# Two gate tiles of a hybrid diffusion trunk multiplied in attention, where identity products stood

## The reference

```python
h = rmsnorm(x, p['norms'][0]) * (1.0 + scale1) + shift1
z = h @ p['w_in']
qa, ka, va, ub, vb, qkvc, bc, ac, zc, gates = jnp.split(z, split_idx, axis=-1)
...
o_a = block_attention(qa, k_all, v_all)
o_b = chunk_gmlp(jax.nn.gelu(ub), jax.nn.gelu(vb), p['gmlp_norm'], p['gmlp_ws'], p['gmlp_bs'])
o_c, s_fin = deltanet_mixer(qkvc, bc, ac, zc, p['dn_conv'], p['dn_a_log'], p['dn_dt_bias'], p['dn_norm'], s0)
g_a, g_b, g_c = jnp.split(jax.nn.sigmoid(gates), N_BRANCH, axis=-1)
...
merged = g_a * (o_a @ wb[0]) + g_b * (o_b @ wb[1]) + g_c * (o_c @ wb[2])
```

## Time and profile before

| | us |
|---|---|
| median of 3 executions | 1819.18 (1812.81 to 1821.51) |
| the profiled execution | 1815.65 |
| its span | 1813.5 |
| PE busy | 1755.4 (97%) |
| DVE, ACT, POOL busy | 1020.1, 790.3, 257.7 |

### The profile page before, as it was taken

How to read it: one execution, slowest core, us unless ns; L and a number is a source line. 1 busy time by engine, 2 the same in 40 slices (tenths; PEclk the granted TensorE clock), 3 DMA queues, 4 the chain that set the end, 5 groups by cost and what they waited for, 6 DMA issues and landing times.

```text
span 1813.5 us, 32205 instructions
## 1 busy us (share of the span) xinstructions
PE 1755.4 (97%) x13983; PEld 1462.4 (81%) x13983; DVE 1020.1 (56%) x1379; ACT 790.3 (44%) x1108; POOL 257.7 (14%) x228
## 2 busy tenths in 40 slices
PE   5999999999999999999999999999999999999997
PEld 4889788987979999888898788887978555556885
DVE  2866645444745344326965545545748544345887
ACT  3355732234335233225366523235356433335775
POOL 2620033241000000003500223330002000000001
PEclk9999999999999999999999999999999999999999
DMA  9661152216453434337541323127567988979994
GB/s 359 202 246 59 52 218 71 95 48 231 142 208 105 139 100 132 139 132 284 189 171 53 124 100 118 48 89 237 216 222 259 364 307 319 343 276 389 385 379 197
DMA packets 175189, 351.27 MB, mean 194 GB/s; under 512 B 5161, under 2 KB 60481, under 8 KB 174544
## 3 DMA queue, kind: packets, MB, share of 16 engines
q1 hardware_dynamic: 170880, 334.50, 51.8%
q0 software_dynamic: 4176, 14.82, 2.3%
HBM read 320.46 MB, written 28.84 MB: 193 GB/s over the span
## 4 chain that ended last, share of the span: by engine, by line
PE 81%; DMA 6%; DVE 5%; ACT 4%; issue 2%; POOL 1%; SPq 0%; POOLq 0%; DVEq 0%; ACTq 0%
PE bank L1806 6%; PE bank L1195 6%; PE bank L1197 5%; PE bank L1196 5%; PE bank L1666 3%; PE bank L1668 3%; PE bank L1782 3%; PE bank L1667 3%; PE bank L1235 3%; PE bank L1783 3%; PE bank L1785 3%; PE bank L1237 3%; PE bank L1236 3%; PE bank L1614 2%; PE bank L1119 2%
## 5 line engine op out<-in xcount | busy, mean ns | idle before, releaser
L1965 ACT ACTIVATE ring_split<-ring 128x1024 fp32r<-128x1024 f32 (+2 forms) x84 | 119.2, 1447 | 178.2 <-DMA ring<-in_ffn_w_up 101.8
L1197 PE MATMUL bank<-hT_hi,ring_split 128*128 128x384 f32 x576 | 193.4, 336 | 0.0
L2884 DVE TENSOR_TENSOR ring_split<-ring,ring_split 128x2048 fp32r<-128x2048 f32 (+1 forms) x28 | 73.8, 2670 | 141.5 <-ACT ring_split L1965 141.5
L1195 PE MATMUL bank<-hT_hi,ring_split 128*128 128x384 f32 x384 | 139.8, 364 | 0.7 <-DVE modv L2540 0.5
L1237 PE MATMUL bank<-ring_split,hT_hi 128*128 128x256 f32 x480 | 135.2, 282 | 0.0
L793 DVE TENSOR_TENSOR ring_split<-ring,w_upper_a 128x2048 fp32r<-128x2048 f32 (+2 forms) x54 | 96.4, 1814 | 59.2 <-PE bank L1806 39.4
L1196 PE MATMUL bank<-hT_lo,ring_split 128*128 128x384 f32 x384 | 128.4, 334 | 0.0
L1666 PE MATMUL bank<-hT_hi,ring_split 128*128 128x384 f32 x352 | 119.1, 338 | 0.0
L1668 PE MATMUL bank<-hT_hi,ring_split 128*128 128x384 f32 x352 | 118.6, 337 | 0.0
L1667 PE MATMUL bank<-hT_lo,ring_split 128*128 128x384 f32 x352 | 117.2, 333 | 0.0
L1235 PE MATMUL bank<-w_gran,hT_hi 128*128 128x256 f32 x384 | 107.7, 280 | 1.3 <-ACT ktok L1965 1.3
(11 more groups left out here) (464 smaller groups left out, 4338.4 us busy)
## 6 DMA issues: line engine op xcount, KB each, us to landing
ring<-in_w_in SPq DMA_DIRECT2D x28, 2048.0 KB, 9.3
ring<-in_ada_w SPq DMA_DIRECT2D x24, 2048.0 KB, 8.8
ring<-in_moe_w_down SPq DMA_DIRECT2D x18, 1536.0 KB, 7.7
ring<-in_moe_w_gate SPq DMA_DIRECT2D x26, 1024.0 KB, 6.0
ring<-in_moe_w_up SPq DMA_DIRECT2D x26, 1024.0 KB, 8.7
ring<-in_w_branch SPq DMA_DIRECT2D x8, 1536.0 KB, 11.5
ring<-in_ffn_w_gate SPq DMA_DIRECT2D x11, 1024.0 KB, 5.3
ring<-in_ffn_w_up SPq DMA_DIRECT2D x11, 1024.0 KB, 7.9
```

The costliest lines, as they stand in the source:

```text
L1195: mm(out, hi, hT_hi[:, k], start=k == 0, stop=False)
L1197: last = mm(out, lo, hT_hi[:, k], start=False, stop=k == KT - 1)
L1965: return go(out, in_, ACT.Copy)
```

## The change

`FILL` becomes a table for each pair. In pairs 0 and 1 the spots u1 to u5, uw, ws0 and so0 have one step less each, 8 steps or one tile a pair. The two tiles T_G + 0 and T_G + 1 are multiplied ahead of DeltaNet: 2 steps where layer 0 had 5 identity products and layer 1 none, 6 steps in place of the 8 identity products, and 2 steps in each of `flip(0)` to `flip(3)` in place of 4, 1, 1 and 1 identity products; `flip(4)` loses its one. DeltaNet thus starts with tile 2, pair 1 with tile 9 and pair 2 with tile 16 as before (`G_FIRST`).

ACT makes the upper parts of blocks 0 and 1 ahead of the decay exponentials, block 2 alone ahead of attention, and copies tile 0 there and tile 1 in attention step 5. DVE subtracts blocks 0 and 1 before it normalises the gMLP values and no longer block 0 ahead of the attention loop. Tile 1 goes to bank 1, since bank 0 is in use by attention, and `weigh(4)` waits until bank 1 is read out. SP's text is not touched.

```diff
--- before.py
+++ after.py
@@ -91,9 +91,11 @@
 LAST = len(LEVELS) - 1
 
 
-FILL = ([("head", 8), ("in", 8), ("turn", 6)]
-        + [spot for s in range(1, LAST + 1) for spot in ((f"w{s}", 2), (f"u{s}", 4 if s < LAST else 3))]
-        + [("uw", 3), ("ws0", 3), ("so0", 4), ("ws1", 3)])
+FILL = tuple([("head", 8), ("in", 8), ("turn", 6)]
+             + [spot for s in range(1, LAST + 1) for spot in ((f"w{s}", 2), (f"u{s}", (3 if less else 4) - (s == LAST)))]
+             + [("uw", 3 - less), ("ws0", 3 - less), ("so0", 4 - less), ("ws1", 3)] for less in (1, 1, 0))
+G_EARLY = 2
+G_FIRST = [G_EARLY + sum(units for spots in FILL[:pair] for _, units in spots) // 8 for pair in range(3)]
 MASKED = -30000.0
 
 
@@ -296,8 +298,8 @@
 
         def filled(pair, spot):
 
-            n = 64 * pair
-            for name, units in FILL:
+            n = 8 * G_FIRST[pair]
+            for name, units in FILL[pair]:
                 n += units
                 if name == spot:
                     return n // 8
@@ -611,7 +613,7 @@
 
         def feature_bank(n):
 
-            return B[(n if n < T_G else n + 1) % 2]
+            return B[1 if n == T_G + 1 else (n if n < T_G else n + 1) % 2]
 
         def token_bank(n):
 
@@ -1330,8 +1332,19 @@
                             last = tr(B[b][:, h * P:(h + 1) * P], cv[:, j0 + h, TCOL[t]:TCOL[t] + P])
                         last.then_inc(S["kvt_mm"], 1)
 
-                if layer == 0:
-                    keep_warm(1, 5)
+                nfill = [0]
+
+                def gate_steps(units):
+
+                    for i in range(nfill[0], nfill[0] + units):
+                        n, k = divmod(i, KT)
+                        if k == 0:
+                            wait(pe, "v_lo", layer, 13 + n + 1)
+                            wait(pe, "proj_ev", layer, T_G + n if 0 < n <= G_EARLY else T_G + n - 1)
+                        feature_step(layer, T_G + n, 7 + n // 4, n % 4, k)
+                    nfill[0] += units
+
+                gate_steps(2)
                 wait(pe, "a_ok", layer, 1)
                 pe.wait_ge(cache_in, 48 * (layer + 1))
                 for t in range(NT):
@@ -1352,7 +1365,7 @@
                     last = tr(B[7][:, g * P:(g + 1) * P], wsraw[:, g])
                 last.then_inc(S["tr_mm"], 1)
 
-                keep_warm(1, 8)
+                gate_steps(6)
                 wait(pe, "tr_ev", layer, 6)
                 wait(pe, "v_ok", layer, 1)
                 for t in range(NT):
@@ -1383,8 +1396,8 @@
                     last.then_inc(S["at_s"], 1)
 
                 def flip(i):
-                    if i < 5:
-                        keep_warm(1, 1 if i else 4)
+                    if i < 4:
+                        gate_steps(2)
                     if i:
                         wait(pe, "at_pt", layer, i)
                     for b in range(2):
@@ -1396,6 +1409,8 @@
                 def weigh(i):
                     t, a, x, w = at_step(i)
                     wait(pe, "at_pt", layer, i + 1)
+                    if i == 4:
+                        wait(pe, "proj_ev", layer, T_G + G_EARLY)
                     if i == 8:
                         wait(pe, "at_o", layer, 1)
                     vs = [qkv[:, 0, 768:1024]] if t == 0 else [vcache, qkv[:, 1, 768:1024], qkv[:, 2, 768:1024]]
@@ -1422,18 +1437,9 @@
                     if i >= 3:
                         weigh(i - 3)
 
-                nfill = [0]
-
                 def fill(pair, spot):
 
-                    units = dict(FILL)[spot]
-                    for i in range(nfill[0], nfill[0] + units):
-                        n, k = divmod(i, KT)
-                        if k == 0:
-                            wait(pe, "v_lo", layer, 13 + n + 1)
-                            bank_free(layer, T_G + n)
-                        feature_step(layer, T_G + n, 7 + n // 4, n % 4, k)
-                    nfill[0] += units
+                    gate_steps(dict(FILL[pair])[spot])
                     assert nfill[0] // 8 == filled(pair, spot)
 
                 QUADS = ((0, 0), (1, 1), (0, 1), (1, 0))
@@ -1485,7 +1491,7 @@
                         wait(pe, "at_o", layer, 3)
                     dn_ada = at[("d0", "d1")[pair]] if pair < 2 else ()
                     for n in dn_ada:
-                        bank_free(layer, T_G + 8 * pair + 1)
+                        bank_free(layer, T_G + G_FIRST[pair] + 1)
                         for half in range(2):
                             ada_quad(n, half, 0)
                     if pair:
@@ -2124,6 +2130,8 @@
                     evac(T_UV + t, uB[:, t], ACT.Gelu_apprx_tanh)
                 for m in range(2, 4):
                     upper_w(layer, 6, m)
+                for m in range(2):
+                    upper_w(layer, 7, m)
                 wait(act, "gc_v", layer, 1)
                 go(edec, edec, ACT.Exp)
                 go(egl, egl, ACT.Exp)
@@ -2147,8 +2155,8 @@
                         copy(kTt[:, :, 256 * (i - 3):256 * (i - 2)], v3(B[2 + i][:, :], 2)).then_inc(S["tr_ev"], 1)
                     else:
                         copy(wsT, B[7][:, :]).then_inc(S["tr_ev"], 1)
-                for m in range(3):
-                    upper_w(layer, 7, m)
+                upper_w(layer, 7, 2)
+                evac(T_G, gates[:, 0], width=TOK)
                 go(yhalf, one1, ACT.Exp)
 
                 def mixed(t):
@@ -2176,12 +2184,14 @@
                                accum_out=ars[:, 2 * i + b:2 * i + b + 1]).then_inc(S["at_e"], 1)
                     if i == 0:
                         mixed(2)
+                    if i == 5:
+                        evac(T_G + 1, gates[:, 1], width=TOK)
                     if i >= 7 and i % 4 == 3:
                         t = i // 4 - 1
                         wait(act, "at_pv", layer, 4 * (t + 1))
                         copy(oT[:, 0, :, t * P:(t + 1) * P], v3(B[t % 2][:, :], 4)).then_inc(S["at_o"], 1)
 
-                ngate, nup = [0], [3]
+                ngate, nup = [G_EARLY], [3]
 
                 def gates_of(pair, spot):
 
@@ -2698,6 +2708,7 @@
                 link(v.tensor_copy(gcs, gps[:, :, 0:8]))
                 v.tensor_tensor(edec, gps[:, :, 8:16], gcs, ALU.subtract)
                 v.tensor_copy(egl.rearrange("p t c n -> p t (c n)"), gps[:, :, 16:32]).then_inc(S["gc_v"], 1)
+                lower_gates(2)
                 wait(dve, "v_rt", layer, 1)
                 link(v.reciprocal(vss, vss))
                 for t in range(NT):
@@ -2716,7 +2727,6 @@
                     last.then_inc(S["b_v"], 1)
 
                 n_at = 4 * NT
-                lower_gates(1)
                 for i in range(n_at + 1):
                     if i < n_at:
                         w = P if i < 4 else TOK
```

## The result

| | kernel before | changed kernel |
|---|---|---|
| median, runs of both on the same chip | 1812.99 (1810.24 to 1821.51, 22 runs) | 1823.32 (1819.35 to 1827.81, 22 runs) |
| ratio, 95% interval | | 1.0046 (1.0036 to 1.0056) |
| the profiled execution, its span | 1815.65, 1813.5 | 1827.81, 1825.9 |
| mean granted clock of TensorE in it | 0.995 | 0.988 |

The changed kernel is slower: the interval lies wholly above 1, and 0.0046 of 1813 is 8.3 us.

The account below looks back on a forecast made before the run. PE was taken to bound the kernel, for 81% of the span. The terms summed to +6.3 us in layer 0 and +2.3 in layer 1, +8.6 on the median of 1819.18, so 1828, range 1817 to 1838.

Parts of the forecast that it names:

- Part 1: Ahead of the attention loop: chain to scores(2) starts 0.8 later, is 1.1 shorter; -0.3 us a layer.
- Part 2: Attention loop: gate steps replace identity products in the flips, all on PE's path; +2.3 us a layer.
- Part 3: Layer 1's attention loop: clock stays at 2.4 GHz as in layer 0; -3.0 us, once.
- Part 4: DeltaNet pairs 0 and 1: 8 steps fewer a pair, 0.52 us each; -8.3 us a layer.
- Part 5: Head of pair 0: three DVE subtractions instead of one ahead of ada_take; +2.5 us a layer.
- Part 6: Head of pair 1: turn_m waits on the late load of w10; +7.2 us in layer 0, +6.2 in layer 1.
- rival (b): Load of w10 lands sooner, stalls of some 2.4 and 1.4 us; 1815, no difference; chance 0.12.
- Part 7: PE's clock falls after the new waits at the heads of pairs 0 and 1: 1.2 and 1.7, +2.9 us a layer.
- Rival (a): Load of w10 at pair 1's head causes no stall: -10.6 in all with the clock held, 1808.6; chance 0.10.
- rival (c): Clock falls twice as long after both new waits, layer 1's attention gains nothing: +16, 1835; chance 0.15.
- (d): Early steps stall PE ahead of attention because block 0 is not lowered in time; chance 0.03.

Follow-up runs that it names:

- e6: Kernel before with only the load of w10 moved ahead of the DeltaNet state exchange in SP's text; 1814.56, ratio 1.0003.
- e7: Kernel before with the 5 identity products ahead of the queries' transposes in layer 1 too; 1813.71, ratio 0.9998.
- e4: Changed kernel with unread identity products in its two new waits, 11 in pair 0 and 26 in pair 1; 1819.92, ratio 1.0038.
- e8: The kernel of e4 run once more; 1821.91, ratio 1.0043.
- e1: Changed kernel with splits_by two instead of three above the complete gate tiles throughout pair 1; 1810.8, ratio 0.9978.
- e3: Changed kernel with the load of w10 moved ahead of the DeltaNet state exchange in SP's text; 1804.69, ratio 0.9957.
- e5: Changed kernel with the edits of e2 and e3 together; 1798.64, ratio 0.9915.
- e9: The changed kernel itself run once more beside the kernel before; 1820.28, ratio 1.0049.
- e2: Changed kernel with block 3 prepared earlier (upper part in attention step 8) and ada_take ahead of the remaining subtractions in pair 0; 1812.49, ratio 0.9993.
- e10: Changed kernel with e2's edits and one block less at the head of pair 1 alone, SP's text unchanged; 1800.04, ratio 0.9923.

## Why the prediction came out as it did

1828 was forecast and 1823.3 came; the difference to before was forecast as +8.6 and came as +8.3 by the ratio, +10.3 between the medians. The level was off because the three runs shown had a median of 1819.18, and 22 have 1812.99. I had put 3.5 us on the profiled execution for that; it was already 2.7 above the median of the 22. I had also taken 0.5% as the least that a measurement tells from no change; with 22 runs of each kernel the interval is 0.1% to either side.

Part 1, the start of attention: right. The wait ahead of scores(2) went from 1.71 to 0.82, forecast "about 0.9".

Part 2, the loop: right. From scores(2) to the end of A took 197.60 to 230.30 in layer 0, and takes 197.05 to 232.13: +2.4, forecast +2.3. All of A at full clock is 1.5 longer, which is 2.4 less the 0.9 of the wait.

Part 3, the clock of layer 1: the gain is there, the attribution was too narrow. I read one execution, saw layer 1 at 0.90 and layer 0 at 1.00, and booked -3.0 once. e6 and e7 show that either layer loses it in some executions (A in layers 0 and 1: 35.94 and 38.94, in e6 38.97 and 37.49, in e7 35.97 and 38.96). The mean of A in before's text is 1.76 above its full-clock 35.95, so the gain is 1.8 us a layer, 3.5 in all. e7 rules out the products ahead of the queries' transposes as the remedy. The shorter wait ahead of scores(2) is the likeliest of what is left: 4 falls in 6 loops with 1.71 us, none in 18 with 0.82. It was not changed by itself, so this is argued and not shown.

Part 4, 8 steps fewer a pair: right in E, -4.1 at full clock (e4, e8: 49.81 against 53.88), forecast -4.16. A round of pair 0 goes from 5.24 us (256.51 to 261.75) to 4.72, one step of 0.52; PE in the changed kernel:

```profile
262.76 0.69 PE L1467 MATMUL bank<-work 64*64 64x64 f32 x32
...
267.48 0.69 PE L1467 MATMUL bank<-work 64*64 64x64 f32 x32
```

In C one of the changed kernel's four values is 51.17 instead of 49.6; see the last section.

Part 5, three subtractions ahead of `ada_take`: right place, too cheap. Forecast +2.5 with bounds of 2.3 and 2.9, measured +3.1 (13.97 in e4 and e8 against 10.87). I had halved the pair of 2.77 us. Taken apart, its first subtraction took 1.22 us and its second 1.63, so the second added 2.77 - 1.22 = 1.55, and two of those are the 3.1 that came. The second of that pair in the kernel before, and the second and third of the three in the changed kernel:

```profile
300.98 1.63 DVE L2604 TENSOR_TENSOR ring_split<-ring,ring_split 128x1024 fp32r<-128x1024 f32 x1
```

```profile
238.29 1.64 DVE L2614 TENSOR_TENSOR ring_split<-ring,ring_split 128x1024 fp32r<-128x1024 f32 x1
239.85 1.63 DVE L2614 TENSOR_TENSOR ring_split<-ring,ring_split 128x1024 fp32r<-128x1024 f32 x1
```

The last section has what sets them apart from the first.

Part 6, the late load: right mechanism, shown by e1 and e3 from both sides. Forecast +7.2 and +6.2, measured +6.0 on average in D (5.4 to 6.9; in the profiled execution 5.6 in layer 0 and 6.9 in layer 1, the other way round than forecast). Its chain from ACT's start to `turn_m` took 3.88 and 3.87 us, forecast 4.3: the last multiply and the overlap of ACT and DVE were overrated. The load itself varies: 10.5 us to landing in layer 0 and 11.7 in layer 1, against 11.7 until ACT began in the row that I used. The rule of the Trainium skill (DMA: Bandwidth & Descriptors, "Anatomy of one DMA", about 2.0 us and the bytes at 436 GB/s) gives 6.8 us as an estimate. The page states it for DMAs issued by GpSimd; the prediction left that out, and SyncE issues these. No run has 6.8 us: where w10 leaves ahead of the state's exchange the six loads of e3, e5 and e6 took 7.9 to 8.7 us from issue to landing, and behind the two state loads those of the changed kernel and e9 took 10.2 to 11.7. e3 and the changed kernel, layer 0:

```profile
ring<-in_w_in SPq DMA_DIRECT2D x1, 2048.0 KB, 8.7
```

```profile
ring<-in_w_in SPq DMA_DIRECT2D x1, 2048.0 KB, 10.5
work<-in_state_delta SPq DMA_DIRECT2D x1, 256.0 KB, 3.3
```

So rival (b), a load that lands as by the rule and stalls of 2.4 and 1.4 us, did not come. The loads behind the state loads took some 2 us longer than those ahead of them, but they differ in their place as well, so that this is the state loads' doing is likely and not shown.

Part 7, the clock after the waits: forecast 1.2 + 1.7 a layer, measured 1.7 + 2.1 in the stages. The reason was right (e4 removes it), the size too small, and in the median hardly any of it shows.

That the sum came out within 0.3 us of the ratio is luck, the errors cancelled: per layer part 5 was 0.6 too low and part 7 0.9 too low, part 6 0.7 and parts 1 and 2 together 0.5 too high, and part 3 brought 0.3 more than booked. The mechanisms of parts 5 and 6, which made the sign, are not luck: e1, e2 and e3 show them one by one.

Rival (a), the change without the load's stall, was forecast at -10.6 with the clock held. e3 is that kernel: -7.8 (0.0043 of 1813), with the clock still lost behind pair 0's wait, 1.5 us a layer (B 15.45 on average against 13.97), which makes -10.8 without it. e5 is parts 1 to 4 alone: -0.3 + 2.3 - 8.3 in layer 0 and 3.0 less in layer 1, -15.6 by the prediction's terms, -15.4 measured; that it fits so closely is again partly luck, since e5 loses some 3 us in C (last section) and gains 1.0 in B that no term holds. Of rival (c) the clock after the new waits came in part (3.8 us a layer, against 2.9 booked and 5.1 by the rival), the loss in attention did not. Of (d) nothing came: PE has no wait at the early steps, and its only new waits above 1.5 us are the four at the heads.

## What to carry to other kernels

Work that is moved to fill gaps moves everything that is counted by it: here the lead with which two other engines prepare the next blocks was tied to the number of finished tiles, and one tile more at a spot put a wait on a late load ahead of the exponentials. For each counter that the moved work drives, write down its new value at each spot and ask which instruction now stands in front of which wait. Then put what the bound engine waits for ahead of what merely has to be ready later: that, and either the load's place or the one block, turned a loss of 8 us into a gain of 14 to 15.

## What the runs showed of the hardware

The clock's fall is not a fixed property of a place in the program: behind the same wait of 1.71 us it came in four of six loops, in either layer, and it began over 1 us after PE had taken up work again (e6: busy from 196.8, at 1.00 in the window of 197 and at 0.54 in that of 198). Behind the waits of 3.3 us and more at the heads it came each time: four times in each of the changed kernel's two traces, and twice each in e1, e2 and e3, which keep one of the two waits. One execution says that it can happen, not what it costs on average.

DVE's subtraction of 128 x 1024 took 1.22 us alone, and 1.22 too when it had begun before POOL's multiply, although POOL then worked beside it for up to 0.88 us of that. When it began while POOL was in one of these multiplies it took 1.63 (238.29 and 239.85 in the changed kernel, 300.98 in the kernel before), beside another multiply of POOL's (L1063 in the kernel before, L1065 in the changed one) 1.35 and 1.83. POOL's pair of multiplies took 1.91 us beside one subtraction of DVE's and 2.88 beside two or three. So what counts is which of the two engines is at work when the other begins, and a mean over a group hides it.

In stage C some executions have 1.2 to 1.8 us more, most of it at a product that waits for no semaphore in the text; e5's line:

```profile
252.24 0.44 PE L1197 MATMUL bank<-hT_hi,ring_split 128*128 128x384 f32 x1 [1.22 <-issue]
```

"issue" is time in which the engine waited for nothing that the profile shows. In e2, e5 and e10 it is there in layer 0 at the same step (and with 0.7 us at another product in layer 1), and C is longer by 1.5 in both layers; in the changed kernel and e1 it is in layer 1 only, in e8 in layer 0 only, and in e9, the changed kernel again, nowhere. What it is stays open, but it costs e5 some 3 us in both layers.
